# Four seven-product pairs in a row, their weight sums kept in DRAM, in a float32 kernel of two transformer blocks

## The reference, cut to what matters

```python
    for layer in range(DEPTH):
        h = rmsnorm(x, norm_mix[layer])
        proj = h @ w_in[layer]
        ...
        merged = jax.nn.sigmoid(ga) * (y_a @ w_up_a[layer]) + jax.nn.sigmoid(gb) * (y_b @ w_up_b[layer])
        x = x + merged @ w_out[layer]
        h = rmsnorm(x, norm_ffn[layer])
        x = x + (jax.nn.silu(h @ w_gate[layer]) * (h @ w_up[layer])) @ w_down[layer]
    return rmsnorm(x, norm_final)
```

## Time and profile before

| | |
|---|---|
| median of 3 runs | 721.14 us (720.99 to 721.19) |
| the profiled execution: its own time | 720.66 us |
| its span, first to last instruction | 718.9 us |
| TensorE busy | 709.1 us |
| VectorE busy | 555.8 us |
| ScalarE busy | 424.6 us |
| GpSimd busy | 25.9 us |
| DMA | 152.22 MB, mean 212 GB/s |

### The profile page before, as it was taken

One profiled execution on the slowest core, in us unless ns is written; L12 is line 12 of the kernel. 1 busy time (PEld: TensorE's weight loads), 2 busy tenths in 40 slices (PEclk: granted clock), 3 DMA queues, 4 the chain that ended last, 5 costly groups with the idle time before them and its releaser, 6 DMA issues.

```text
span 718.9 us, 9667 instructions
## 1 busy us (share of the span) xinstructions
PE 709.1 (99%) x3722; PEld 567.9 (79%) x3722; DVE 555.8 (77%) x949; ACT 424.6 (59%) x701; POOL 25.9 (4%) x43
## 2 busy tenths in 40 slices
PE   8999999999999999999999999999999999999996
PEld 4678885588888888888888777778888888888885
DVE  4789999898666757756998799855857988678933
ACT  4487658995754654546645677666456466436712
POOL 1030012001000000000010000000000000000000
PEclk9999999999999999999999999999999999999999
DMA  9996939617556585744548433344375598568501
GB/s 366 415 378 224 387 104 357 218 59 263 197 179 231 214 289 196 268 146 154 163 144 300 172 118 118 119 172 178 118 233 175 197 313 310 181 230 316 209 1 58
DMA packets 71932, 152.22 MB, mean 212 GB/s; under 512 B 4096, under 2 KB 19456, under 8 KB 70864
## 3 DMA queue, kind: packets, MB, share of 16 engines
q1 hardware_dynamic: 70080, 146.32, 57.4%
q0 software_dynamic: 1520, 5.03, 2.0%
q10 hardware_dynamic: 288, 0.27, 0.1%
HBM read 150.56 MB, written 1.05 MB: 211 GB/s over the span
## 4 chain that ended last, share of the span: by engine, by line
PE 91%; ACT 3%; issue 2%; DMA 2%; DVE 1%; POOL 0%; POOLq 0%; DVEq 0%; SPq 0%
PE bank L511 23%; PE bank L513 23%; PE bank L512 23%; PE bank L856 5%; PE bank L493 5%; PE bank L854 3%; DMA W<-in_w_in 2%; ACT WH L1185 1%; PE bank L530 1%; PE bank L988 1%; PE bank L1010 1%; PE bank L694 1%; PE bank L716 1%; PE bank L570 1%; PE bank L853 1%
## 5 line engine op out<-in xcount | busy, mean ns | idle before, releaser
L1720 DVE TENSOR_TENSOR WL<-W,WH 128x1024 fp32r<-128x1024 f32 (+2 forms) x234 | 263.4, 1173 | 27.0 <-ACT WH L1185 26.7
L1185 ACT ACTIVATE WH<-W 128x1024 fp32r<-128x1024 f32 (+2 forms) x234 | 222.9, 1013 | 55.7 <-DMA W<-in_w_mlp 35.8
L511 PE MATMUL bank<-WH,AHL 128*128 128x512 f32 (+1 forms) x440 | 173.1, 393 | 0.0
L513 PE MATMUL bank<-WH,AHL 128*128 128x512 f32 (+1 forms) x440 | 169.7, 386 | 0.0
L512 PE MATMUL bank<-WL,AHL 128*128 128x512 f32 (+1 forms) x440 | 169.6, 385 | 0.0
L511 PEld LDWEIGHTS bank<-WH,AHL 128*128 128x128 f32 x440 | 82.7, 188 | 19.0 <-issue 3.2
L513 PEld LDWEIGHTS bank<-WH,AHL 128*128 128x128 f32 x440 | 82.6, 188 | 16.9
L512 PEld LDWEIGHTS bank<-WL,AHL 128*128 128x128 f32 x440 | 82.8, 188 | 15.4
L511 PE MATMUL bank<-WH,HH 128*128 128x512 f32 (+1 forms) x218 | 84.9, 390 | 0.0
L513 PE MATMUL bank<-WH,HL 128*128 128x512 f32 (+1 forms) x218 | 84.5, 388 | 0.0
L512 PE MATMUL bank<-WL,HH 128*128 128x512 f32 (+1 forms) x218 | 84.4, 387 | 0.0
(11 more groups left out here) (307 smaller groups left out, 937.8 us busy)
## 6 DMA issues: line engine op xcount, KB each, us to landing
W<-in_w_mlp SPq DMA_DIRECT2D x32, 1024.0 KB, 5.4
W<-in_w_in SPq DMA_DIRECT2D x24, 1024.0 KB, 5.1
W<-in_w_down SPq DMA_DIRECT2D x11, 1024.0 KB, 5.1
W<-in_w_ada SPq DMA_DIRECT2D x10, 1024.0 KB, 8.0
WX<-in_w_ada SPq DMA_DIRECT2D x10, 1024.0 KB, 10.0
W<-in_w_out SPq DMA_DIRECT2D x8, 1024.0 KB, 5.2
W<-in_w_up SPq DMA_DIRECT2D x8, 1024.0 KB, 5.1
W<-in_w_gate SPq DMA_DIRECT2D x14, 512.0 KB, 4.0
```

Source lines behind the costliest of these rows:

```text
L511: e.matmul(po, hs, wh[:, k, c0:c0 + cw], start=first and k == 0, stop=False, skip_group_check=onto)
L513: ins = e.matmul(po, ls, wh[:, k, c0:c0 + cw], start=False, stop=last and k == unit.nk - 1, skip_group_check=onto)
L1185: e.activation(m.WH[unit.slot][:, c], m.W32[unit.slot][:, c], ACT.Copy).then_inc(S["w_hi"], 1)
L1720: e.tensor_tensor(m.WL[unit.slot][:, c], m.W32[unit.slot][:, c], m.WH[unit.slot][:, c].bitcast(F32), ALU.subtract).then_inc(S["w_lo"], 1)
```

## The change

`PAIRS` becomes (2, 4, 6, 8): chunks (2,3), (4,5), (6,7) and (8,9) are pairs, with plain chunks 0, 1 before and 10 behind. All four pairs are `STORED`: their weight sums aren't made in the ring but earlier, from w_up_2 and w_gate_2, in sixteen steps, and kept in a DRAM tensor `sums`; the ring's units for the four sums of a pair are then loaded from there.

A step s works on one of the places `sums` (8 KB a partition): POOL issues two loads of 0.5 MB each (`blocks_in`), DVE does four subtractions of 128x512 (`kept_sums`), POOL issues a store of 1 MB. Steps 0 to 9 alternate between two places, steps 10 and 11 use one place, steps 12 to 15 alternate between two. A place's next load waits for its store's landing. `SUMS_AT` tells how many steps stand at each of thirteen places of DVE's program: 0 to 6 in the first MLP (ten steps; two each at places 2, 3 and 6), 7 and 8 among the projections (place 8 directly ahead of the index sums), 9 and 10 in the merge, 11 within the norm of the first row half, 12 ahead of the norm features of the second. DVE waits for outstanding stores (`sums_stored`) at three places where their buffers are used again, one of them after the gated rows of the first chunks.

In the feed-forward part PE now turns the pair's first row half between the next pair's first and second product, and its second row half behind the second. ACT, where a pair follows, copies both hidden halves ahead of the last `hi(2)`; DVE interleaves the low halves of hidden rows and weights. The input sums are formed earlier. Semaphores res1, res2, res3 become one.

```diff
+        self.sums = {o: M(f"sums{o}", o, [128, 4, 512]) for o in (0, 8, 68, 76)}
...
-PAIRS = (3,7)
+PAIRS = (2, 4, 6, 8)
+STORED = (2, 4, 6, 8)
+STEPS = (10, 2, 4)
+SUMS_AT = (1, 1, 2, 2, 1, 1, 2, 1, 1, 1, 1, 1, 1)
+SUMS = [[(0, 8)[s % 2] for s in range(STEPS[0])], [0] * STEPS[1], [(68, 76)[s % 2] for s in range(STEPS[2])]]
+SUM_SEM = [{0: 0, 8: 1, 68: 0, 76: 1}[o] for phase in SUMS for o in phase]
+SUM_AT = [48 * sum(b == SUM_SEM[s] for b in SUM_SEM[:s]) for s in range(len(SUM_SEM))]
...
+        if GROUPS[g][0] in STORED and n in (1, 2, 4, 6):
+            s = STORED.index(GROUPS[g][0])
+            kept = d["sums"][s, {4: 0, 2: 1, 1: 2, 6: 3}[n]].rearrange("p (k n) -> p k n", k=4)
+            units[-1].pieces = [(0, 512, kept)]
+            units[-1].kept = [(S[f"l_sums{SUM_SEM[i]}"], SUM_AT[i] + 48) for i in range(4 * s, 4 * s + 4)]
...
+    def blocks_in(phase, i):
+        s = sum(STEPS[:phase]) + i
+        place, landing = m.sums[SUMS[phase][i]], S[f"l_sums{SUM_SEM[s]}"]
+        if SUM_AT[s]:
+            w.wait_ge(landing, SUM_AT[s])
+        if i < 2 and phase == 0:
+            w.wait_ge(*((S["n_turned"], 4), (S["kn"], 4))[i])
+        elif phase == 1:
+            w.wait_ge(S["n_turned"], 8)
+        elif phase == 2:
+            w.wait_ge(S["pv2"], 8)
+        c0, kt = 256 * STORED[s // 4], s % 4
+        for j, src in enumerate(("w_up_2", "w_gate_2")):
+            rows = d[src][:, c0:c0 + 512].rearrange("(h k p) n -> p k h n", h=2, p=128)[:, kt, :, :]
+            e.dma_start(place[:, 2 * j:2 * j + 2, :], rows).then_inc(landing, 16)
+    def kept_sums(phase):
+        ahead = len(set(SUMS[phase]))
+        for i in range(ahead):
+            blocks_in(phase, i)
+        for i in range(STEPS[phase]):
+            s = sum(STEPS[:phase]) + i
+            w.wait_ge(S["made"], 4 * s + 4)
+            kept = d["sums"][s // 4, :, :, 512 * (s % 4):512 * (s % 4) + 512].rearrange("i p n -> p i n")
+            e.dma_start(kept, m.sums[SUMS[phase][i]][:, :, :]).then_inc(S[f"l_sums{SUM_SEM[s]}"], 16)
+            if phase == 2 and i in (1, 2):
+                power(9 + i)
+            if i + ahead < STEPS[phase]:
+                blocks_in(phase, i + ahead)
 
     e.dma_start(m.vec[:, :], d["vec"]).then_inc(S["l_vec"], 16)
...
+    kept_sums(0)
...
-    for i in range(10, 14):
-        power(i)
+    kept_sums(1)
+    kept_sums(2)
+    power(12)
+    power(13)
...
-    def begin(g):
+    def begin(g, between=lambda: None):
         if GROUPS[g][1]:
             part(by["gu", g][0], m.AH, m.AL, 0, 0, 4, True, True, "gu_mm", n_ready(2, 0))
+            between()
...
     for g in range(2, NG - 1):
         rest(g)
-        if GROUPS[g][1]:
+        if GROUPS[g][1] and GROUPS[g + 1][1]:
+            begin(g + 1, lambda: hid_turn2(g, 0))
+            hid_turn2(g, 1)
+        elif GROUPS[g][1]:
             begin(g + 1)
...
-    up2(NG - 1, 0)
+    if not GROUPS[NG - 2][1]:
+        up2(NG - 1, 0)
...
-        hi(2)
+        if not GROUPS[g + 1][1]:
+            hi(2)
+        for tb in range(2):
+            hid_hi2(g, tb)
+        if GROUPS[g + 1][1]:
+            hi(2)
...
+    if GROUPS[2][1]:
+        for i in range(4):
+            form_hi(i)
...
+    def sums_stored():
+        for b in range(2):
+            w.wait_ge(S[f"l_sums{b}"], max([0, *(SUM_AT[s] + 48 for s in range(made["n"]) if SUM_SEM[s] == b)]))
+    def kept_sums(place):
+        for s in range(sum(SUMS_AT[:place]), sum(SUMS_AT[:place + 1])):
+            at = m.sums[sum(SUMS, [])[s]]
+            u0, u1, g0, g1 = (at[:, i, :] for i in range(4))
+            w.wait_ge(S[f"l_sums{SUM_SEM[s]}"], SUM_AT[s] + 32)
+            tt(g0, u0, g0, ALU.subtract, "made")
+            tt(u0, u1, u0, ALU.subtract, "made")
+            w.wait_ge(S["made"], 4 * s + 1)
+            tt(u1, u1, g0, ALU.subtract, "made")
+            w.wait_ge(S["made"], 4 * s + 3)
+            tt(g1, g1, u1, ALU.subtract, "made")
+            made["n"] = s + 1
+    made = {"n": 0}
     hid_lo(0, 4, 0, 1)
     lo(2)
...
             gate_add()
+        kept_sums(c)
...
 
+    sums_stored()
...
     features2(2, two(m.qiT, 1))
     lo(2)
+    kept_sums(7)
...
     features2(6, two(m.qbT, 1))
     lo(2)
+    kept_sums(8)
...
     w.wait_ge(S["p2_turned"], 10)
+    sums_stored()
...
     merge_a(1, 0)
     merge_a(1, 1)
+    kept_sums(9)
...
     merge_b(1, 0)
     merge_b(0, 1)
+    kept_sums(10)
...
-    residual(0, 1, "out2_mm", 7, "res2")
+    norm_features(4, 0, m.ffn, None, lambda: kept_sums(11))
...
     norm_scale(1, 11, (18, 19))
     lo()
+    kept_sums(12)
...
+        def first_hidden():
+            w.wait_ge(S["hid_turned"], 4 + 2 * (g - 2) + 2)
+            w.wait_ge(S["silu"], SILU_AT[g, 0])
+            w.wait_ge(S["quad"], 5 * q + 4)
+            tt(m.hid[g % 2][:, 0, :], m.u0, m.rel[0][:, :], ALU.mult, "hid2")
+
+        if near:
+            first_hidden()
         w.wait_ge(S["gu_mm"], QUAD_AT[g] + 7)
         tt(m.g1[:, :], bank[6][:, :], m.g1[:, :], ALU.add, "quad")
         if following:
             make(g + 1, 1)
         lo()
-        w.wait_ge(S["hid_turned"], 4 + 2 * (g - 2) + 2)
-        w.wait_ge(S["silu"], SILU_AT[g, 0])
-        w.wait_ge(S["quad"], 5 * q + 4)
-        tt(m.hid[g % 2][:, 0, :], m.u0, m.rel[0][:, :], ALU.mult, "hid2")
+        if not near:
+            first_hidden()
         w.wait_ge(S["silu"], SILU_AT[g, 1])
         tt(m.hid[g % 2][:, 1, :], m.u1, m.rel[1][:, :], ALU.mult, "hid2")
-        lo(2)
+        if near:
+            hid_lo2(g, 0)
+            lo()
+            hid_lo2(g, 1)
+            lo()
+        else:
+            lo(2)
+            for tb in range(2):
+                hid_lo2(g, tb)
 
     norm_features(5, 1, m.ffn, None)
...
     gated(0, 0)
     gated(1, 0, 0)
-    lo()
+    sums_stored()
+    if GROUPS[2][1]:
+        form(0)
+        form(1)
+        lo()
+        form(2)
+        form(3)
+    else:
+        lo()
     gated(0, 1)
     hid_lo2(0, 0)
     lo(2)
     gated(1, 1, 1)
     hid_lo2(0, 1)
-    lo()
-    for i in range(4):
-        form(i)
+    if GROUPS[2][1]:
+        for i in range(4):
+            form_lo(i)
+        lo()
+    else:
+        lo()
+        for i in range(4):
+            form(i)
     for tb in range(2):
         hid_lo2(1, tb)
```

More of the change, by code:

```diff
@@ L313, in weight_units @@
             quad_unit(g, 6, "w_gate_2", 1)
-            b11, t1, t2, b22, t3, b21, t4 = by["gu", g]
-            loads += [b11, t1, t2, *down, t4, b22, t3, b21]
+            if kept:
+                loads += units[first:]
+            else:
+                b11, t1, t2, b22, t3, b21, t4 = by["gu", g]
+                loads += [b11, t1, t2, *down, t4, b22, t3, b21]
             continue
@@ L359, in weight_units @@
         unit.lo = (S["w_lo"], 2 * u)
-    for n, g in enumerate(g for g in range(NG) if GROUPS[g][1]):
+    for n, g in enumerate(g for g in range(NG) if GROUPS[g][1] and GROUPS[g][0] not in STORED):
         t1, t2, _, t3, _, t4 = by["gu", g][1:]
@@ L363, in weight_units @@
             unit.base = unit.landed
[L364 removed]
+        t1.landed, t2.landed, t4.landed, t3.landed = ((S["made"], 4 * len(SUM_SEM) + 8 * n + 2 * i + 2) for i in range(4))
     return units, loads, by
@@ L383, in load @@
             w.wait_ge(old.free[0], old.free[1])
+        for sem, value in unit.kept:
+            w.wait_ge(sem, value)
         v = unit.block(m)
@@ L1677, in scalar_program @@
             hi()
-        for tb in range(2):
-            hid_hi2(g, tb)
+            for tb in range(2):
+                hid_hi2(g, tb)
     hi()
@@ L2523, in vector_program @@
             lo()
-        for tb in range(2):
-            hid_lo2(g, tb)
+            for tb in range(2):
+                hid_lo2(g, tb)
     lo()
```

97 lines of the change are left out of this document (57 added, 40 removed).

## The result

The changed kernel takes 764.7 us (median of 4 runs, 762.4 to 765.5) against 721.1 us: the ratio is 1.060 with a 95% interval of 1.058 to 1.062. It is slower, as forecast, but by 43.6 us and not by 26.6: 764.7 lies above the range of 730 to 758. Its profiled execution took 765.48 us with a span of 763.7, which is 44.8 us over the span before.

A forecast was written before the change was run, and what follows sets the result against it. The prediction took TensorE, busy 99% of the span, to bound the kernel. Its terms, -5.4 + 4.7 + 3.5 + 3.7 + 16.0 + 4.1 = +26.6 on 721.1, gave 747.7 us, range 730 to 758.

The forecast's parts named there:

- What is saved: Feed-forward pairs: two more pairs save 2 x 12 matmuls of 0.227 us each, -5.4 us, all on the path.
- Steps 0 to 9: First MLP: 26 us of DVE subtractions fit in 49.2 us of DVE idle, so cost 0.
- The allowance of 3 us for late transfers at the doubled places: First MLP, three places with two steps: up to 3 us if a transfer were late and the idle used up.
- POOL's transfers are late everywhere: Rival, chance 0.05: 14 us or more for store and load, in the MLP too, stalls DVE; 760 us or more.
- hardly any PE idle in the first MLP: Sign that the forecast is right: TensorE would have almost no idle time in the first MLP.
- Step 11, +4.7: Ahead of the index sums: store then load through one place delay DVE, ACT's relus and PE by 4.7 us.
- The lower bound of 1.4: Index sums: the step there costs +1.4 us if its load is in time.
- Steps 12 and 13, +3.5: In the merge: DVE's subtractions delay the last addition and the merged rows' low half for PE, together +3.5 us.
- step 15, +3.7: Before the last norm's first low half: subtractions, then DVE's wait for the store, delay PE; +3.7 us, bounds 1.5 and 5.
- Boundaries, +16.0: Three pair-to-pair boundaries: ACT splits down weights behind both hidden copies, so PE waits; 5.3 us each, +16.0 us.
- Last boundary, +4.1: From the last pair to the plain chunk: PE asks earlier for the hidden low half; +4.1 us, bounds 3.6 and 5.
- The clock falls: Rival, chance 0.12: new PE waits each followed by as long a stretch at 1.2 GHz, +9.1, so 756.8 us.

The follow-up runs named there:

- The three pairs: Two kernels with three pairs instead of four, eight and four stored steps, all in the first MLP: 718.9 and 718.6 us; kernel before 721.1.

## Why the prediction was right or wrong

- *What is saved*: right. The pairs last 24.6 us and the spans bear out 2.3 to 3 us a pair.
- *Steps 0 to 9, "26 us of DVE work in 49.2 us of DVE idle, so 0"*: the step that failed, and the largest error, 12.8 us, alone enough to leave the range. It has two faults. The idle was summed, not sorted: some 16 us of it belong to a chain and can't be used. And the transfers were priced from a stage with DMA share 0.64 and from single loads of 4 to 6.2 us; with the steps the share is 0.92 there, stores landed after 9 to 13 us, and VectorE stood 10.4 us for loads. Neither costs much alone: subtractions without transfers cost 0.3 us, transfers with short subtractions 1.7. The allowance of 3 us for late transfers at the doubled places named the right spots and was too small. The rival "POOL's transfers are late everywhere" (0.05) named this mechanism; it deserved far more, since it only had to be true where two steps stand at one place of VectorE's program. The sign "hardly any PE idle in the first MLP" failed with it: 8.7 us, released by VectorE, which had stood for a POOL load.
- *Step 11, +4.7*: right in mechanism (6.5 + 6.7 us of transfers, TensorE waits 3.8 where 4.0 was worked out) and 1.3 short: 424 to 428 us has a clock of 0.71. In eight other profiles the stage cost 6.5 to 7.4 us, so the size was under by up to 2.7. The lower bound of 1.4 for a load in time was too high; it measured 0.2. By my estimate of 4.4 us a transfer from the Trainium skill ("DMA: Bandwidth & Descriptors", Anatomy of one DMA) the step would have cost 1.4; the 6.5 and 6.7 us measured beside other traffic speak against it.
- *Steps 12 and 13, +3.5; step 15, +3.7*: 3.7 and 3.7 (the second up to 4.8 in other profiles). The three pairs show that of the second, nothing comes from forming the input sums earlier by itself.
- *Boundaries, +16.0*: the mechanism was right in each part, and the size to 0.1 us a pair where the clock stays up. In the changed kernel's profile the term is 4.2 too small, since I let the clock stay at 1.00 behind waits of 3 us; in three of the four other profiles with these waits it is 0.4 to 0.6 too small, with the clock low behind most of them.
- *Last boundary, +4.1*: 4.1 in the changed kernel's profile, 5.1 to 5.4 in the seven where the clock fell behind the wait. So the forecast holds for the clock of 1.00 that it took.
- *The clock falls* (0.12): it did. In the changed kernel matmuls are 0.427 us apart from 625.8 to 630.1, in place of 0.227, and the same behind the MLP's waits of 3.6 and 3.9 us and behind the 3.8 at the index scores. At the boundaries it cost 4.1 us there and 0.3 to 2.6 in the other profiles; the rival had 9.1 for all places, as if every such stretch cost half of its length. For the MLP, 12.8 - 8.6 = 4.2 us are left once the waits are taken off. By the granted clock some 3.4 us of them are the clock (an estimate: from 278 to 284 us it was 0.72, 0.50 and 0.93 in stretches of 2 us, from 330 to 334 it was 0.52 and 0.63); no run tests it. By the rule of the Trainium skill ("TensorE: Matmul & The Clock Gate", HAM oscillation) idle gaps bring half clock, and at most of the long waits the trace agrees (0.427 us a matmul). As a forecast of its own it would have given 756.8, nearer than mine, but more by luck than by its reason: most of what was lacking was the MLP.

The five terms that I put on the path were there, in the changed kernel's profile each within 1.3 us but for the clock at the boundaries. Of the 18 us that were lacking 12.8 came from a stage that I had booked at nothing, and most of the rest from the clock.

## What to carry to other kernels

Sort an engine's idle time by what ends it before you spend it: idle inside a chain of its own isn't free, and new work in the rest also has to be at its place in time. A step that loads, works and stores through one buffer has a period of store + load, and both grow with the traffic that the steps themselves add; of two such steps in a row at one place of an in-order program, the second stalls everything behind it when its load isn't there. Where splits, copies and turns of one boundary stand in one queue, order them by when TensorE asks for them: here that alone was worth 18 of 44 us. And look at the same wait in several profiles before you put a price on what follows it: one profile gave 4.1 us for three waits that cost 0.3 to 0.5 in most others.
